# The tap products of GpSimd's convolution tiles made by ScalarE, in a one-core two-block kernel on Trainium2

## What is computed

```python
def centred_dwconv(x, w, b):
    pad = (CONV_K - 1) // 2
    L = x.shape[1]
    xp = jnp.pad(x, ((0, 0), (pad, pad), (0, 0)))
    out = xp[:, 0:L] * w[0]
    for tap in range(1, CONV_K):
        out = out + xp[:, tap:tap + L] * w[tap]
    return out + b
...
    proj = jnp.einsum('bld,dp->blp', n, w_in)
    conv_in, gates, scal = jnp.split(proj, [CONV_CH, CONV_CH + GATE_CH], axis=-1)
    c = jax.nn.silu(centred_dwconv(conv_in, conv_w, conv_b)).astype(F32)
```

## Time and profile before

| | us |
|---|---|
| median of 3 runs | 1369.34 |
| lowest and highest | 1368.98, 1369.68 |
| the profiled execution, its own time | 1367.08 |
| its span, first to last instruction | 1364.8 |
| convolution stage on ScalarE, first copy to last SiLU | 31.0 to 171.4 |
| TensorE without work between its last projection and `kq_decay(0)` | 9.64 |

### The profile page before, as it was taken

The page is one execution under the profiler, slowest core; times in us unless marked ns, Lnnn a source line. Parts: engine busy times, 40 slices in busy tenths (PEclk is TensorE's granted clock), DMA queues, the critical chain, the costliest instruction groups (busy, mean ns, idle before and its releaser), DMA issues.

```text
span 1364.8 us, 17988 instructions
## 1 busy us (share of the span) xinstructions
PE 1223.3 (90%) x7446; PEld 921.9 (68%) x7446; DVE 642.1 (47%) x1059; ACT 409.3 (30%) x990; POOL 327.8 (24%) x322
## 2 busy tenths in 40 slices
PE   6999799899999699978779998998988999899887
PEld 5888665577844322212129898997878889798777
DVE  1776866232640300001035354575787255456785
ACT  4447341132722400100024521311514441230332
POOL 0665731211200300000022022232253112223231
PEclk8999899899999799999999998999999999899899
DMA  5343244757216799999972435153332344335310
GB/s 197 126 155 142 82 145 153 248 194 283 79 62 246 284 420 421 421 421 421 422 298 78 155 124 189 65 183 124 124 112 86 115 171 169 112 106 183 124 62 31
DMA packets 91555, 257.02 MB, mean 188 GB/s; under 512 B 7646, under 2 KB 12535, under 8 KB 79059
## 3 DMA queue, kind: packets, MB, share of 16 engines
q1 hardware_dynamic: 89122, 248.67, 48.7%
q0 software_dynamic: 2032, 6.95, 1.6%
q10 hardware_dynamic: 320, 0.26, 0.1%
HBM read 253.49 MB, written 2.12 MB: 187 GB/s over the span
## 4 chain that ended last, share of the span: by engine, by line
PE 67%; DMA 14%; DVE 7%; ACT 6%; POOL 3%; issue 2%; SPq 1%; DVEq 0%; ACTq 0%; POOLq 0%
PE bank L686 64%; DMA ring<-in_w_up_dram 8%; DMA ring<-in_w_down_dram 4%; PE bank L695 3%; DVE ring_r L1996 3%; POOL late L2605 2%; POOL acc L2606 1%; DMA ring<-in_w_ada_dram 1%; ACT ring L1511 1%; ACT cT L1511 1%; ACT oa L1511 1%; ACT L1511 1%; ACT qkT L1511 1%; ACT xT L1511 0%; DVE nmx L2455 0%
## 5 line engine op out<-in xcount | busy, mean ns | idle before, releaser
L2708 POOL CAST w_hi_r<-ring 128x1024 fp32r<-128x1024 f32 x136 | 150.9, 1138 | 669.5 <-DMA ring<-in_w_in_dram 267.2
L686 PE MATMUL bank<-ring_r,xT_hi 128*128 128x256 f32 (+1 forms) x864 | 245.4, 284 | 0.0
L686 PE MATMUL bank<-w_hi_r,xT_hi 128*128 128x256 f32 x704 | 208.3, 296 | 24.1 <-DVE ring_r L1996 19.7
L1996 DVE TENSOR_TENSOR ring_r<-ring,w_hi_r 128x1024 fp32r<-128x1024 f32 x136 | 182.6, 1375 | 42.0 <-POOL w_hi_r L2708 42.0
L686 PE MATMUL bank<-w_hi_r,xT_r 128*128 128x256 f32 x704 | 201.9, 287 | 0.0
L686 PEld LDWEIGHTS bank<-ring_r,xT_hi 128*128 128x128 f32 x864 | 167.9, 194 | 0.2
L686 PEld LDWEIGHTS bank<-w_hi_r,xT_hi 128*128 128x128 f32 x704 | 136.8, 194 | 36.4 <-DVE ring_r L1996 25.7
L686 PEld LDWEIGHTS bank<-w_hi_r,xT_r 128*128 128x128 f32 x704 | 136.6, 194 | 0.0
L686 PE MATMUL bank<-ring,xsT 128*32 128x512 f32 x496 | 111.8, 595 | 26.3 <-DMA ring<-in_w_up_dram 13.2
L686 PE MATMUL bank<-xT,ring 128*128 128x256 f32 x576 | 127.5, 384 | 0.0
L686 PEld LDWEIGHTS bank<-xT,ring 128*128 128x128 f32 x576 | 110.9, 193 | 15.4
(11 more groups left out here) (360 smaller groups left out, 2124.3 us busy)
## 6 DMA issues: line engine op xcount, KB each, us to landing
ring<-in_w_in_dram SPq DMA_DIRECT2D x39, 2048.0 KB, 7.8
ring<-in_w_up_dram SPq DMA_DIRECT2D x32, 1024.0 KB, 16.3
ring<-in_w_down_dram SPq DMA_DIRECT2D x32, 1024.0 KB, 16.3
ring<-in_w_gate_dram SPq DMA_DIRECT2D x30, 1024.0 KB, 16.3
ring<-in_w_ada_dram SPq DMA_DIRECT2D x12, 2048.0 KB, 9.3
ring<-in_w_out_dram SPq DMA_DIRECT2D x8, 2048.0 KB, 7.8
ring<-in_w_o_mla_dram SPq DMA_DIRECT2D x2, 2048.0 KB, 12.7
ring<-in_w_o_swa_dram SPq DMA_DIRECT2D x2, 2048.0 KB, 7.7
```

Of the source, the lines that this page charges most:

```text
L686: return release(nc.tensor.matmul(o, lhsT, rhs, start=start, stop=stop))
L1996: tt(lo, raw_, hi.bitcast(F32), ALU.subtract).then_inc(lo_done.sem, lo_done.one("piece"))
L2708: nc.gpsimd.tensor_copy(hi, raw_).then_inc(hi_done.sem, hi_done.one("piece"))
```

## The change

ScalarE makes the six products of each of GpSimd's tiles, right behind tap 0 of that tile, as six activations with the tap's weight as scale. They go into six buffers of their own, which fill the first three quarters of `late` (nothing else uses it in this stage). A new semaphore counts them. GpSimd has only the adds left, and each waits for its product and the add before it. Before the products of a tile, ScalarE waits until GpSimd is through with its previous tile.

```diff
             yint = late
+            conv_products = late_all[:].rearrange("p a (b n) -> p (a b) n", n=T)
...
         conv_pool = Steps(sem("conv_pool"), "tile")
+        conv_prod = Steps(sem("conv_prod"), "tap")
...
                 f(acc[:, i, :], raw[:, i, 0:T], ACT.Identity, scale=cols[:, V_CW + n:V_CW + n + 1],
                   bias=cols[:, V_CB + n:V_CB + n + 1]).then_inc(conv_tap0.sem, 1)
+                if n in conv_mine(True):
+                    if conv_mine(True).index(n):
+                        act.wait_ge(conv_pool.sem, conv_mine(True).index(n))
+                    for j in range(1, CONV_K):
+                        f(conv_products[:, j - 1], raw[:, i, j:j + T], ACT.Copy, scale=tap(n, j)
+                          ).then_inc(conv_prod.sem, conv_prod.one("tap"))
                 if n >= 3:
                     conv_silu(n - 3)
...
-            prod = late[0][:].rearrange("p (a n) -> p a n", a=2)
-            for n in conv_mine(True):
+            for i, n in enumerate(conv_mine(True)):
                 pool.wait_ge(conv_tap0.sem, n + 1)
                 for j in range(1, CONV_K):
-                    link(nc.gpsimd.tensor_scalar(prod[:, j % 2], raw[:, n % 4, j:j + T], tap(n, j), None, ALU.mult))
-                    ins = nc.gpsimd.tensor_tensor(acc[:, n % 4, :], acc[:, n % 4, :], prod[:, j % 2], ALU.add)
+                    pool.wait_ge(conv_prod.sem, i * (CONV_K - 1) + j)
+                    ins = nc.gpsimd.tensor_tensor(acc[:, n % 4, :], acc[:, n % 4, :], conv_products[:, j - 1], ALU.add)
                     if j < CONV_K - 1:
                         link(ins)
                 ins.then_inc(conv_pool.sem, 1)
```

## The result

| | before | changed |
|---|---|---|
| first comparison, median | 1369.16 (4 runs) | 1360.08 (4 runs: 1356.94 to 1361.8) |
| ratio, 95% interval | | 0.9941 (0.9925 to 0.9957) |
| profiled execution, span | 1364.8 | 1355.1 |
| three later series of the changed kernel, 12 runs each | 1366.55, 1366.92, 1366.92 | 1363.97, 1363.19, 1363.58 |
| their ratios | | 0.9976 (0.996 to 0.9993), 0.9973 (0.9958 to 0.9988), 0.9977 (0.9964 to 0.9991) |

The first comparison gave 9.1 us, far outside the range of the prediction (1364.3 to 1369.4). The later series, each on one chip with the kernel before beside it, gave 2.6, 3.7 and 3.3 us; the second and third stand against the same 23 runs of before. The two kinds of figure have intervals that just fail to meet, and both have to be explained. The kernel is faster by any of them.

The account below looks back on a forecast made before the run. The prediction held that ScalarE, GpSimd and VectorE, not TensorE, bound the convolution stage's end. Gates 4.4 us earlier minus 2.2 us of TensorE's half clock gave 2.2 us: 1369.34 - 2.2 = 1367.1 us, range 1364.3 to 1369.4.

Parts of the forecast that it names:

- The place and what is late next: End of convolution stage: ScalarE's SiLUs stop waiting for GpSimd (24.0 us); VectorE's work is late next, then TensorE.
- ScalarE's price: ScalarE's six products take 2.5 us per tile, 2.4 to 3.1 at the ends; on the path only at tile 23.
- The 2.5 us won and given back: Tiles 22 to 24: SiLU of tile 19 starts 2.5 us earlier, tile 23's products take that; VectorE's tile 24 stays at 130.7.
- VectorE's ten tiles: From tile 24, VectorE's 60 instructions take 30.9 us plus 13 adds at 0.40, 5.2 us; end at 166.8, 4.1 us earlier.
- The sum: Whole forecast: gate block 4.4 us earlier, less 2.2 us for TensorE's half clock, gives 2.2 us.
- TensorE behind it: TensorE stops nearly 7 us before head 4; gates start 4.4 us earlier, less 2.2 us (1.6 to 2.9) for half clock.
- Taken against the median it is 1369.34 - 2.2: Whole kernel: the 2.2 us gain subtracted from the median of the runs of before gives 1367.1 us.
- should reach the end whole: Behind the gate blocks: the 2.2 us shift passes undiminished to the kernel's end.
- price of 0.85: By the skill's lock rule, each GpSimd add costs VectorE its whole length, 0.85 us; the sum ends 5.9 us later, 1373.0.
- (D): Rival, slower: GpSimd's adds starve VectorE for whole tiles, 0.95 us per add; kernel takes 1374.3 us; chance 0.07.
- (C): Rival, gain eaten by dearer or slow products, growing add gaps or a late inverse: 0 to 1.4 us gain; chance 0.25.
- (B): Rival, full gain: adds catch VectorE less often, or clock recovers before head 4; 4.4 to 5.7 us gain; chance 0.18.

Follow-up runs that it names:

- double_23: Changed kernel, with ScalarE making six more products at tile 23 behind the real ones, into memory nothing reads then; 1365.1 us, ratio to before 0.9991.
- double_27: Changed kernel, with ScalarE making six more products at tile 27 behind the real ones, into memory nothing reads then; 1363.14 us, ratio 0.9987.
- no_adds_tail: Changed kernel, with only the last tap added in GpSimd's tiles 27 and 31, five adds each left out; 1363.15 us median in 12 runs.
- late_products: Changed kernel, with the products of a GpSimd tile made one step later, behind tap 0 of the next tile; median 1365.65 us, ratio to before 0.9994.
- exp_early: Changed kernel, with SiLUs of tiles 34 and 35 after the exponentials, ahead of the first gate block's SiLU; 1358.48 us, ratio 0.9939; again 1357.89, 0.9941.

## Why the prediction was wrong

Point by point, by its own steps:

- **The place and what is late next: right.** No SiLU waits for GpSimd; TensorE's first head is released by the last copy, 1.8 us after its last projection (1.0 forecast).
- **ScalarE's price: right.** 2.49 us for six (2.5), 493 ns each alone. It was right that it counts at tile 23 and not behind it: double_23 and double_27 show both, and at tile 31 VectorE works on without a wait.
- **The 2.5 us won and given back: right.** Tile 24 starts 14.37 us after the copy of tile 22, 14.50 before.
- **VectorE's ten tiles: mis-sized by 1.5 us.** The sum had 30.9 + 5.2 = 36.1 from a start of 130.7; it took 34.56. The instructions beside adds were 0.83 to 0.95, as forecast, but only the 12 adds of tiles 27 and 31 stood beside them, since tile 23's were done in 4.75 us, as tile 24 began. The 5.7 us that the prediction had for them came from an add beside VectorE (0.85); with VectorE quiet the six take 4.75 with their gaps. The price was 0.34 instead of 0.40, and the 60 instructions by themselves take 30.45 instead of 30.9 (no_adds_tail).
- **TensorE behind it: right in kind, mis-sized by 0.4.** From the exponentials to the gates it took 11.4 us, in the sum 9.6 + 2.2 = 11.8, and before it was 10.0. The stop was 4.3 us, not 7, since VectorE's end was 1.7 us earlier than forecast and the first head began 0.8 us later. The clock stayed at half for 3.4 us, not 4.4:

```profile
161.80:166.00 4.20, 0.00 (x0) 0.00 (x0) 1.32 (x3) 4.17 (x12) 0.00 (x0) 1.00 0.47 174
166.60:170.00 3.40, 3.40 (x18) 3.30 (x17) 3.29 (x6) 2.30 (x9) 0.00 (x0) 0.50 0.02 5
```

  Together the stage gave 4.4 us where the sum had 2.2.
- **"Taken against the median it is 1369.34 - 2.2", and the range: this step failed.** The sum and its range had no term for what differs between executions of the same kernel; it was put at nothing without a reason. I took the spread from three runs of before, 0.7 us wide, and read the stage in one profiled execution. The later 94 runs of before lie between 1360.42 and 1372.31, with series' medians of 1365.8 to 1366.9 instead of 1369.34, and 36 of the changed kernel between 1356.55 and 1367.47. The walk before the stage and the part behind it move by up to 5.6 and 3.2 us from one execution of a kernel to the next, with the time that TensorE spends at half clock. With the mechanism sized exactly the forecast would have been 1364.9, inside the range and still 4.9 us above what was measured first. Read as a gain, the range was 0 to 5.0 us; the first comparison's 9.1 lies outside it, the later 2.6, 3.7 and 3.3 inside. That the shift "should reach the end whole" is not contradicted, but shown only as far as these three reach: 3.3 us with an error of 0.5, of 4.4.
- **The rivals.** The Trainium skill, "SBUF — State Buffer", "Who interferes with whom", has a VectorE instruction with two inputs in SBUF and a GpSimd instruction that reads SBUF lock each other out for a whole instruction. By the price of 0.85 that the prediction works out for that, the kernel would have been slower. One VectorE instruction does wait for each add, as the rule has it, but it ends 0.28 us after the add did, less than its own 0.48, and the next add starts 0.08 us after the last; a pair takes 0.87 us and not 0.48 + 0.72. The price is 0.34 and not 0.85. (D) is out: VectorE was never starved. So is (C): the products took what was forecast and the gaps between adds did not grow. (B) was nearest, and partly by luck: fewer adds did meet VectorE, as it says, but the clock's loss that it leaves out was there.

What stays open: why the first four runs of before lay within 0.9 us of each other at 1368.8 to 1369.7 when later ones scatter over 12 us, and so how much of the first 9.1 us belongs to that chip or that moment. By the scatter of the later runs, a difference of two sets of four has an error of 1.7 us, so 9.1 lies over three such errors above 3.3; mere scatter between executions hardly gives that. The three later comparisons, two of which share their runs of before, agree with each other and, at the edge of their error, with the stage. That the remaining difference of about a microsecond between 4.4 and 3.3 us is chance was not shown.

## What to carry to other kernels

Work that is moved to an engine costs where that engine is waited for: the same six products were free at one tile and cost their full 2.5 us at another, so walk the chain tile by tile instead of comparing busy shares. When a slow helper is taken off the path, look at once for the floor behind it; here TensorE's pace was only 0.35 us away, and what helped further was not a faster engine but taking two tiles that nothing there reads out of the chain. And count a stage from an instruction ahead of the change in both traces, since two spans can differ by more than the change is worth; where a view prints a full clock, check it against the lengths of the matmuls.

## What the hardware did that I had not expected

- The same program on the same inputs took from 1360.4 to 1372.3 us. In the profiled executions up to 5.6 us of that lie in the first 28 us, where TensorE ran at half clock for nothing, for 6.8 us or for all of the time that the clock has no record of. Behind the gates the executions with 55 to 59 us at half clock took 2.6 to 4.4 us less than those with 69 to 72.
- A stop of TensorE of 4.25 us brought a stretch at half clock of 3.4 us, in all five executions that had it (the four of the changed kernel and double_27); it began between 0.4 us before and 0.6 us after TensorE had work again. After a stop of 5.4 us (late_products) it was 6.8 us, of which 5.1 fell on work, and after one of 6.8 us (double_23) 6.8, of which 4.2 did. After one of 1.24 us (exp_early) there was none.
- VectorE and GpSimd, both with two inputs in SBUF, settle into one instruction each per 0.87 us when both are busy without pause; VectorE's takes 0.83 to 0.95 instead of 0.48, and GpSimd's six adds 5.1 to 5.3 us instead of 4.75.
